# Stage entries of a two-block transformer kernel: two more places for split weights, four tiles that go with their input, the norm's sum inside a fifth tile

## The reference

```python
def reference(x, ...):                       # x: 1 x 256 tokens x 2048
    x = first_block(x, ...)                  # linear attention + windowed attention, then experts
    return second_block(x, ...)

def second_block(x, p, ...):
    for i in range(2):
        h = rmsnorm(x, g_pre[i])
        uz = jnp.einsum('bsd,de->bse', h, w_in[i])          # 2048 -> 8192
        u, z = uz[..., :D_INNER], uz[..., D_INNER:]
        if i % 2 == 0:
            y = pool_mixer(u, ...)           # trailing means of 2, 4, 8, 16 tokens, then 1024 x 1024 maps
        else:
            y = rglru(causal_depthwise_conv(u, ...), ...)   # gates, then a recurrence over tokens
        y = y * jax.nn.silu(z)
        o = jnp.einsum('bse,ed->bsd', y, w_out[i])          # 4096 -> 2048
        x = x + rmsnorm(o, g_post[i])
        gate = jax.nn.sigmoid(jnp.einsum('bsd,de->bse', rmsnorm(x, g_ple_in[i]), w_ple_gate[i]))
        e = jnp.einsum('bsk,kd->bsd', p[i], w_ple[i])       # 256 -> 2048
        x = x + rmsnorm(e * gate, g_ple_out[i])
    return x
```

## Time and profile before

| | |
|---|---|
| median of 3 runs | 3526.09 us (3519.31 to 3535.12) |
| profiled execution | 3514.12 us, span in the trace 3512.8 us |
| PE busy | 3417.8 us, 97% |
| DVE busy | 2267.9 us, 65% |
| ACT busy | 1653.0 us, 47% |
| DMA | 668.66 MB, 190 GB/s |
| granted TensorE clock, mean | 0.991 of 2.4 GHz |

### The profile page before, as it was taken

One profiled execution on the slowest core, in us unless ns is written; L12 is line 12 of the kernel. 1 busy time (PEld: TensorE's weight loads), 2 busy tenths in 40 slices (PEclk: granted clock), 3 DMA queues, 4 the chain that ended last, 5 costly groups with the idle time before them and its releaser, 6 DMA issues.

```text
span 3512.8 us, 66401 instructions
## 1 busy us (share of the span) xinstructions
PE 3417.8 (97%) x29340; PEld 3380.5 (96%) x29340; DVE 2267.9 (65%) x2940; ACT 1653.0 (47%) x1771; POOL 250.8 (7%) x196
## 2 busy tenths in 40 slices
PE   8999999999999999999999999999998799999988
PEld 8899999999999999999999989999998799999987
DVE  5676679885555555545555578778546677876455
ACT  4444344455544444344444443333445567766454
POOL 0000000378800000000000000000000000000000
PEclk9999999999999999999999999999999899999999
DMA  6434455555576666655666545555554355555543
GB/s 240 144 132 167 158 217 183 181 201 216 197 247 216 217 219 220 213 196 196 205 216 218 194 168 192 192 194 191 193 193 142 136 181 191 192 193 191 192 144 132
DMA packets 123887, 668.66 MB, mean 190 GB/s; under 512 B 10512, under 2 KB 44048, under 8 KB 45648
## 3 DMA queue, kind: packets, MB, share of 16 engines
q1 hardware_dynamic: 86688, 622.65, 50.3%
q10 hardware_dynamic: 36912, 41.75, 3.5%
HBM read 643.39 MB, written 20.97 MB: 189 GB/s over the span
## 4 chain that ended last, share of the span: by engine, by line
PE 68%; DVE 4%; ACT 3%; issue 2%; DVEq 0%; ACTq 0%
PE PS L463 22%; PE PS L464 22%; PE PS L465 22%; ACT WH L927 2%; DVE WL L1394 1%; PE PS L763 1%; DVE A L1405 0%; DVE XT L1968 0%; DVE EE L1965 0%; ACT SQ L941 0%; DVE UCS L2019 0%; DVE TMP L1567 0%; DVE OO L1418 0%; PE PS L505 0%; DVE XT L1790 0%
## 5 line engine op out<-in xcount | busy, mean ns | idle before, releaser
L1394 DVE TENSOR_TENSOR WL<-RAW,WH 128x2048 fp32r<-128x2048 f32 x589 | 1349.7, 2292 | 943.1 <-ACT WH L927 942.5
L463 PE MATMUL PS<-A,WH 128*128 128x256 f32 x5648 | 1600.1, 283 | 40.9 <-DVE A L1405 32.2
L464 PE MATMUL PS<-A,WH 128*128 128x256 f32 x5648 | 1573.8, 279 | 0.0
L465 PE MATMUL PS<-A,WL 128*128 128x256 f32 x5648 | 1573.3, 279 | 0.0
L927 ACT ACTIVATE WH<-RAW 128x2048 fp32r<-128x2048 f32 x589 | 1127.1, 1914 | 862.1 <-PE PS L465 843.1
L463 PEld LDWEIGHTS PS<-A,WH 128*128 128x128 f32 x5648 | 1069.9, 189 | 64.3 <-issue 28.4
L464 PEld LDWEIGHTS PS<-A,WH 128*128 128x128 f32 x5648 | 1069.2, 189 | 3.6 <-issue 2.6
L465 PEld LDWEIGHTS PS<-A,WL 128*128 128x128 f32 x5648 | 1071.9, 190 | 0.0
L463 PE MATMUL PS<-CO,WH 128*128 128x256 f32 x2048 | 565.3, 276 | 0.0
L465 PE MATMUL PS<-CO,WL 128*128 128x256 f32 x2048 | 565.3, 276 | 0.0
L464 PE MATMUL PS<-CO,WH 128*128 128x256 f32 x2048 | 565.3, 276 | 0.0
(11 more groups left out here) (258 smaller groups left out, 2684.0 us busy)
## 6 DMA issues: line engine op xcount, KB each, us to landing
RAW<-in_w_in SPq DMA_DIRECT2D x177, 1024.0 KB, 4.7
RAW<-in_peer_down SPq DMA_DIRECT2D x128, 1024.0 KB, 4.8
RAW<-in_peer_up SPq DMA_DIRECT2D x128, 1024.0 KB, 5.3
RAW<-in_w_out SPq DMA_DIRECT2D x80, 1024.0 KB, 4.7
RAW<-in_w_gate SPq DMA_DIRECT2D x32, 1024.0 KB, 4.7
RAW<-in_w_query SPq DMA_DIRECT2D x16, 1024.0 KB, 4.8
gates_away<-XT ACTq DMA_DIRECT2D x16, 1024.0 KB, 5.8
RAW<-in_pool_w SPq DMA_DIRECT2D x16, 1024.0 KB, 4.8
```

Of the source, the lines that this page charges most:

```text
L463: e.matmul(ps, wh, x[:, k, 0, :], start=first, stop=False, skip_group_check=True)
L464: e.matmul(ps, wh, x[:, k, 1, :], start=False, stop=False, skip_group_check=True)
L465: return e.matmul(ps, wl, x[:, k, 0, :], start=False, stop=last, skip_group_check=True)
L1394: e.tensor_tensor(WL[:, c % NSPL, :], RAW[:, c % NRAW, :], WH[:, c % NSPL, :].bitcast(F32), ALU.subtract).then_inc(s_lo, 1)
```

## The change

- `WX0` and `WX1` are two further places for a high and a low part, in memory that `Y` uses at other times. Table `EXTRA` sends seven chunks there: the second of the pool stage, the second and third of each gate stage, the second and fourth of the recurrent stage. The other chunks go round the three old places, counted without those seven; `W_BEFORE` is the chunk whose use frees a place. `RAW` stays as it was.
- `entering` follows a list of steps (first block, end block, tiles). Four tiles go with A's blocks, and the norm's sum is asked after block 8 of a fifth tile. In the pool and recurrent stages the fifth tile has bank 5.
- The conversions are put at other places in ACT's and DVE's programs. In the gate stages DVE scales, multiplies and adds first and then makes weights for three tiles ahead (it was two, and first). After the last gate tile fewer conversions are left; those of the next stage stand at tiles 13 and 14.
- The update of x in the gate stages is in six pieces (it was five). In the up projection's end, the low part of the second pool chunk is made a step earlier, and two low parts of A follow each update of x (it was one).
- ACT loads the table and makes the first gate chunk's high part between the last square and the logarithm; after the last gate tile the norm stands ahead of the last gain, and DVE waits for the gains piece by piece.
- The first sum of E is asked a pair of matmuls earlier.

```diff
+EXTRA = {C_L[0] + 1: 0, C_G[0] + 1: 0, C_G[0] + 2: 1, C_L[1] + 1: 0, C_L[1] + 3: 1, C_G[1] + 1: 0, C_G[1] + 2: 1}
...
+    for x in range(2):
+        place["at"] = base + 4096 + 2048 + 30720 * x + 64
+        WX.append(put(f"WX{x}", [128, 2, 2048], FR))
...
+    for c in range(NCH):
+        s = ("extra", EXTRA[c]) if c in EXTRA else (c - sum(x < c for x in EXTRA)) % NSPL
+        W_HIGH.append(WX[EXTRA[c]][:, 0, :] if c in EXTRA else WH[:, s, :])
+        W_LOW.append(WX[EXTRA[c]][:, 1, :] if c in EXTRA else WL[:, s, :])
+        W_BEFORE.append(last_in.get(s))
+        last_in[s] = c
...
-                plan_dve(c, k % 4)
+                plan_dve(c, (0, 1, 2, 3, 5)[k] if k < 5 else (k - 5) % 4)
...
+    ENDS = [(12, 16, (i,)) for i in range(4)]
+    POOL_ENTRY = [(0, 14, (0, 1)), (14, 16, (0,)), (14, 16, (1,)), (0, 16, (2,)), (0, 16, (3,))]
+    GATE_ENTRY = [(0, 4, (0,)), (0, 4, (1,)), (4, 8, (0, 1)), (0, 8, (2,)), (8, 12, (0, 1, 2)), (0, 12, (3,))] + ENDS
+    LRU_ENTRY = [(0, 12, (0, 1, 2, 3))] + ENDS
...
+    ENTRY_LEAD = (5, 6, 6, 7)
+
+    GATE_LEAD = {i: (i + 3, i + 3) for i in range(4, 13)} | {13: (17, 17), 14: (19, 18)}
...
+    def entering(e, m, N, c0, steps):
+        ready = -1
+        for k0, k1, tiles in steps:
+            for k in range(k0, k1):
+                for i in tiles:
+                    if k == 0:
+                        wait_bank(e, c0 + i)
+                        e.wait_ge(s_lo, c0 + i + 1)
+                    if k > ready:
+                        e.wait_ge(s_al, 16 * N + k + 1)
+                        ready = k
+                    ins = block(e, psum(c0 + i), c0 + i, k, A, k, k == 0, k == 15)
+                    if k == 15:
+                        ins.then_inc(s_used, 1)
+        for b in tile(e, c0 + 4, A):
+            if b == 8:
+                summed(e, m)
...
     def up_dve(e, p):
...
-            lo_to(e, C_UP[p] + jj + 2)
+            if p == 0 or jj < n - 1:
+                lo_to(e, C_UP[p] + jj + (3 if p == 1 and jj == n - 2 else 2))
...
             if p == 1 and q:
-                a_low(e, 2, q - 1, vec("g_pre_2", q - 1))
+                for k in (2 * q - 2, 2 * q - 1):
+                    a_low(e, 2, k, vec("g_pre_2", k))
+            if p == 1 and q == 4:
+                lo_to(e, C_L[0] + 2)
...
     def dve_pool(e):
...
-                if g or x > 1:
-                    lo_to(e, c + 2)
+                lo_to(e, c + 2 if g or x > 3 else c0 + ENTRY_LEAD[x])
...
     def dve_ple(e, l):
...
+        lo_to(e, C_G[l])
         e.wait_ge(s_r, 2 * (3 + 4 * l) + 2)
         update(0)
         update(1)
-        lo_to(e, C_G[l])
         lows(0)
+        lows(1)
         lo_to(e, C_G[l] + 1)
-        lows(1)
         update(2)
+        update(3)
         lows(2)
-        update(3)
+        lows(3)
         lo_to(e, C_G[l] + 2)
-        lows(3)
         update(4)
+        lo_to(e, C_G[l] + 3)
         lows(4)
+        update(5)
+        lo_to(e, C_G[l] + 4)
+        lows(5)
...
     def dve_gate(e, l):
...
+        lo_to(e, c0 + 6)
         for i in range(16):
-            if i >= 3:
-                lo_to(e, c0 + i + 2)
             if i >= 2:
                 e.wait_ge(s_gm, 16 * l + i - 1)
             scaled(e, c0 + i, TMP[:, i % 2, :], m - 1)
             if i:
                 mul(i - 1)
             if i >= 3:
                 add_square(e, m, i - 2)
+            if 4 <= i < 15:
+                lo_to(e, c0 + GATE_LEAD[i][1])
...
     def act_gate(e, l):
...
         for i in range(16):
-            if i >= 3:
-                hi_to(e, c0 + i + 2)
+            if 4 <= i < 15:
+                hi_to(e, c0 + GATE_LEAD[i][0])
             sig(i)
...
         sqr(15)
+        norm(e, m)
         gain(15)
-        norm(e, m)
```

More of the change, by code:

```diff
@@ L453, in sp_program @@
         o4 = out.rearrange("p (k t) -> p k t", k=KD)
-        for q, (k0, k1) in enumerate(LAST_PIECES):
-            e.wait_ge(s_upd, 15 + q + 1)
+        for q, (k0, k1) in enumerate(PIECES["last"]):
+            e.wait_ge(s_upd, UPD["last", 1] + q + 1)
             e.dma_start(o4[:, k0:k1, :], XT[:, k0:k1, :]).then_inc(s_out, 16)
@@ L879, in pe_lru @@
         c0 = C_L[1]
-        entering(e, 6, 4, c0)
+        entering(e, 6, 4, c0, LRU_ENTRY)
         for g in range(8):
@@ L924, in hi @@
         e.wait_ge(s_raw[c % NRAW], 16 * (c // NRAW + 1))
-        if c >= NSPL:
-            e.wait_ge(s_used, c - NSPL + 1)
-        e.activation(WH[:, c % NSPL, :], RAW[:, c % NRAW, :], ACT.Copy).then_inc(s_hi, 1)
+        if W_BEFORE[c] is not None:
+            e.wait_ge(s_used, W_BEFORE[c] + 1)
+        if c == C_L[0] + 1:
+            e.wait_ge(s_cl, n_coef[1, 23])
+        for l in range(2):
+            if c in (C_G[l] + 1, C_G[l] + 2):
+                e.wait_ge(s_used, C_E[l])
+        e.activation(W_HIGH[c], RAW[:, c % NRAW, :], ACT.Copy).then_inc(s_hi, 1)
     def hi_to(e, c):
@@ L1258, in act_ple, with high @@
         c0, N, gain = C_G[l], 3 + 2 * l, ("g_ple_in_2", 16 * l)
-        hi_to(e, c0)
-        a_high_piece(e, N, 10 * l + 1, 0, 2, gain)
+        def high(x):
+            a_high_piece(e, N, UPD["gate", l] + x + 1, *PIECES["gate"][x], gain)
         hi_to(e, c0 + 1)
-        a_high_piece(e, N, 10 * l + 2, 2, 4, gain)
+        high(0)
+        high(1)
         e_out(e, l, 0)
-        a_high_piece(e, N, 10 * l + 3, 4, 8, gain)
+        hi_to(e, c0 + 2)
+        high(2)
+        high(3)
         e_out(e, l, 1)
-        hi_to(e, c0 + 2)
-        a_high_piece(e, N, 10 * l + 4, 8, 12, gain)
-        a_high_piece(e, N, 10 * l + 5, 12, 16, gain)
+        hi_to(e, c0 + 3)
+        high(4)
+        high(5)
+        hi_to(e, c0 + 4)
     def act_gate(e, l):
@@ L1961, in dve_gate @@
         add_square(e, m, 15)
+        if l == 0:
+            lo_to(e, c0 + 19)
         e.wait_ge(s_r, 2 * m + 2)
-        e.wait_ge(s_eg, 16 * l + 16)
-        for x, (k0, k1) in enumerate(PIECES if l == 0 else LAST_PIECES):
+        stage = ("last", "lru")[l == 0]
+        for x, (k0, k1) in enumerate(PIECES[stage]):
+            e.wait_ge(s_eg, 16 * l + k1)
             e.tensor_tensor(EE[:, k0:k1, :], EE[:, k0:k1, :], R[:, :].unsqueeze(1).broadcast_to([128, k1 - k0, T]),
```

124 lines of the change are left out of this document (50 added, 74 removed).

## The result

| kernel | median, us | runs | profiled execution | its span |
|---|---|---|---|---|
| before, beside it | 3530.61 (3519.31 to 3536.11) | 4 | 3514.12 | 3512.8 |
| after | 3481.56 (3474.13 to 3484.89) | 4 | 3481.15 | 3479.8 |

The ratio is 0.9862, 95% interval [0.9831, 0.9894]: 1.4% faster. The forecast was 3483, range 3465 to 3503. That is a difference of 38.2, which is the better figure. Two runs of later kernels (b1 and b2) took 15896 and 5549 us, were disturbed, and are left out of every figure.

The account below looks back on a forecast made before the run. PE was taken as the bound, busy 97% of the span, with 95 us at most from idleness. Gains 12.1 + 4.4 + 12.5 + 1.0 + 13.0 = 43.0 us gave 3471 profiled, 3483 on the median; range 3465 to 3503.

Parts of the forecast that it names:

- Pool entry: Start of the pool stage: tile 8 starts at 2079 instead of 2080.05, a gain of 1.0 us (-3 to +2).
- The PE lead of 6 us is handed back as two waits: Pool stage's entry: PE's earlier start is lost again in waits of 4.3 us before tile 5 and 3.5 before tile 8.
- First gate stage: From the last output tile to the last gate tile's end: no gap at the sum, 5.44 us a tile, gain 12.1 us.
- The 1.6 us allowed for the clock: First gate stage: 1.6 us added for one stretch at the lower clock and tiles somewhat slower after a wait.
- If the loop stayed at 5.80, 4.0 less: First gate stage: if conversions still came every 5.80 us a tile, the gain of 12.1 would be 4.0 us less.
- Between the stages: From the last gate tile's end to DVE's first use of R: 10.3 us becomes 5.9, gain 4.4 us (2.5 to 5).
- recurrent entry: From R to the recurrent stage's tile 8: +64.9 us becomes +52.4, with a wait of 2.7; gain 12.5 us (8.5 to 15).
- Second gate stage: Same instructions as the first, but it lost one stretch more to the clock: gain 13.0 us (8 to 15).
- Tail: The part after the second gate stage's last tile: stays as it was, no gain.
- Entries lose clock: Rival: eight half-clock stretches at the chopped entries cost 10 us more, gain 33, time 3493 us; chance 0.14.
- The stalls only move: Rival: R comes mid-tile and the backlog behind it grows, as in the pool stage; gain 15, time 3511 us; chance 0.10.
- Slower by interleaving: Rival: four interleaved tiles at the entries take twice 0.113 us a matmul, costing 77 us, time 3560; chance 0.03.

Follow-up runs that it names:

- b1: The kernel after, with the pool stage's first six tiles asking for splits so that tile 8's halves are made one tile earlier: 3481.38 us, ratio 0.9868.
- b2: The kernel after, with the sum ahead of the fifth tile, the entries' settling transposes behind the sum, and b1's pool lead: 3466.79 us, ratio 0.9835.
- a0: The kernel after, unchanged, timed and profiled again: 3481.99 us, ratio 0.9906 to the kernel before.
- b0: The kernel after, with the gate loops' old order restored except for the conversions at tiles 13 and 14: 3486.69 us, ratio 0.9892 to the kernel before.
- a1: The kernel after, with the four entries' settling transposes moved from tile 4 to tile 5, 8 or 9: 3475.37 us, ratio 0.9865 to the kernel before.
- b3: b2 with settling transposes at six further places, in stretches the change does not touch: 3464.72 us, ratio 0.9828 to the kernel before.
- a2: The kernel after, with the norm's sum ahead of the fifth tile instead of within it: 3469.41 us, ratio 0.9856 to the kernel before.

## Why the prediction was right, step by step

Its mechanism held in the main, and its sum of 43.0 us stands against 39.9 in the same parts. That 3483 lies so near to 3481.6 is in part luck. The saving of 43.1 was taken from a median of 3526.1; from the 3520.0 of 66 runs it would have given 3477, and the saving by all runs is 38.2. Of the signs that were named, the conversions came every 5.65 us and not 5.44, and matmuls in an entry were over 0.113 us apart without a wait, which had been named as a sign of being wrong. The interval of 3466 to 3498 does not follow from its bounds either: gains of 24 and 51 with 0.2% give 3468 to 3509.

- *Pool entry*, forecast 1.0, measured 0.2 (1.0 in a0). The walk put waits of 4.3 and 3.5 us before tiles 5 and 8; they came there with 3.93 and 1.70. "The PE lead of 6 us is handed back as two waits" is what the rows show. The logarithm is 27.3 us behind the end of the up projection, forecast 26.8. Tile 8 starts 54.8 behind it, forecast 55.0 and before 56.0; the longer pace in tiles 8 to 11 then gave 0.9 back. In b0 tile 8 starts 54.3 behind it, with a wait of 3.25: the low part sets the start, and the wait takes up what the clock leaves.
- *First gate stage*, forecast 12.1, measured 10.5. A chopped entry, no wait at the sum and a PE that is not held were right. The 1.6 us allowed for the clock and for "tiles that run somewhat slower after a wait" was the mis-sized term: the longer pace alone cost 2.2 to the stage's end, and no clock was lost. Without it (a1, b2, b3) the stage takes 106.8 to 106.9, a gain of 12.6.
- *If the loop stayed at 5.80, 4.0 less*: this step failed. b0 has the loop at 5.79 and loses nothing inside the stage, and 3.4 at the first sum, though with PE at the long pace.
- *Between the stages*, forecast 4.4, measured 5.1 (8.10 to 3.00), and *recurrent entry*, forecast 12.5, measured 12.3: from DVE's first use of R at 2769.74 to tile 8 at 2822.32 are 52.6 us, forecast 52.4, before 64.9. Its wait was 1.28, not 2.7, and the weights' DMA was late as forecast (the wait of 1.51 for RAW).
- *Second gate stage*, forecast 13.0, measured 11.1, again the pace. *Tail*, forecast 0, measured 0.5.
- The parts do not add. The loop alone gives 10.6 to 14.9 us, all but the loop 33.9 (b0 against before), both 39.9. With the old entry the loop holds PE; with the new one it hardly does.
- *What the 39.9 us are made of.* In the four changed parts ahead of the tail PE's idle time fell from 51.6 to 24.2 us. The granted clock was at 0.50 for 47.8 us of these parts before and for 17.1 after. 144 matmuls started in that time before, 52 after; at 0.21 instead of 0.113 us each, that is some 9 us. The last 3 or 4 us are what the loop no longer holds, less the longer pace. The prediction named the waits of 4.4, 4.1, 8.1 and 4.3 us as the gaps at the entries; those of 4.62 at the sums and one of 3.39 (at 2791.01) were of like size, and its walks removed them without counting them as such.

**The rivals.** *Entries lose clock*: refuted for the kernel after, which had two stretches at half clock and not eight, but not for the entries as such. Windows of PE in the kernel after: the gate entry, the pool stage behind its wait of 3.93 us, and with all engines the stretch from the last gate tile to tile 8 and the second gate stage (0.82 and 0.96 before):

```profile
2661.00:2700.00 39.00, 34.00 (x283) 1.00 0.43 145
...
2061.00:2066.00 5.00, 4.56 (x21) 0.50 0.60 210
```

```profile
2764.40:2822.30 57.90, 49.35 (x396) 48.23 (x394) 45.87 (x67) 35.71 (x63) 0.00 (x0) 0.91 0.32 115
3354.00:3463.30 109.30, 104.52 (x876) 103.30 (x874) 72.11 (x90) 68.56 (x108) 0.00 (x0) 1.00 0.39 136
```

And in the first gate entry of a2, behind its wait of 1.94 us:

```profile
2678.00:2681.00 3.00, 3.00 (x16) 3.00 (x16) 2.97 (x5) 0.00 (x0) 0.00 (x0) 0.50 0.92 306
```

Four waits of 0.48 to 1.84 us in 39 us left the granted clock at 1.00, the 2.4 GHz level; behind one wait of 3.93 us it was 0.50, the 1.2 GHz level. But waits of the same lengths did not always leave it alone. Nine profiles have the new gate entries, 18 in all. In five of them (one in a1, both in a2, one in b1, one in b2) the granted clock fell to 0.50 for 3.4 us, within 1.5 us of the end of the wait of 1.84 or 1.94. So the kernel after drew none of these stretches, and they cost some 1.5 us where they came. The Trainium skill ("TensorE: Matmul & The Clock Gate", section "HAM oscillation — how this bites in real kernels") tells of a kernel with bursts of about 2 us and waits of 3 to 5 us for DMAs, which is re-throttled at every wait. The row behind 3.93 us agrees; the waits of the gate entries are shorter than that, and the clock fell behind some of them and not behind others. *The stalls only move*: true for the pool stage, where 5.6 us of waits stand for one of 4.4, and false elsewhere. *Slower by interleaving*: refuted; the matmuls of the four interleaved tiles of the recurrent entry start 0.11 us apart once the clock is back. In the pool entry they start 0.118 apart from 2035 on, which costs 0.6 us there; the rival needed 0.056 us more each.

## What to carry to other kernels

Give each engine of a loop the step that another one waits for first, and the conversions for later tiles last. In the kernel before that order alone was worth 10 to 15 us by the stage tables. Undone in the kernel after it cost 3.4 us in the stages: what a loop's order is worth depends on how far ahead its engines enter it. When an entry is reordered, look at what comes next in the order of DVE: in the pool stage the six rounds behind R took back what four early tiles had won, and moving the sum ahead of the fifth tile won 2 to 4 us of it again, part of it as clock, with a wait for the sum of 0.3 us at most (b3). Time a change of one part together with its stage rows: one kernel gave 0.9996 and 0.9943 in timings on two chips, their medians 17 us apart, while its changed parts agreed within 5 us.

## What was not expected of the hardware

The two paces, 0.1133 and 0.1178 us a matmul, both at granted clock 1.00. Over the fourteen profiles the longer one cost 12 to 42 us of an execution. Of 237 groups of four settling transposes with a running stream on both sides, 97 came in the longer pace and 85 of these left it; 140 came in the shorter one and 14 of these lost it; other interruptions (the sum in full float32, a wait) change it too. Why a stream takes the one or the other stays open: DMA load does not tell them apart (0.54 and 187 against 0.54 and 192 GB/s in the windows above), and nothing in the code does in the untouched stretches. The Trainium skill, "TensorE: Matmul & The Clock Gate", section "Back-to-back issue gap", gives a sustained spacing of about 81 ns for streams of weight loads and matmuls of 128 columns and of about 131 ns for 512. Both paces here, 113 and 118 ns with 256 columns, lie between; no run here measures the other two.

The other thing is that the same waits can cost clock in one execution and none in the next: behind the gate entries' waits of about 1.05, 0.48 and 1.84 us the granted clock fell in 5 of 18 entries.
